# A one-core hybrid decoder layer: TensorE without extra transposes of the identity in its first waits

## The reference

```python
h = concatenate([meta_tokens, x])                 # 528 x 1024
hn = rms_norm(h, norm_mix_gain)
q, k, v, fg, glu_in, gate_a, gate_c = split(hn @ w_in)   # 3*1024, 16, 2048, 1024, 1024
a = forgetting_attention(q, k, v, fg + b_forget) @ w_attn_out
u = glu_in[:, :1024] * sigmoid(glu_in[:, 1024:])
c = silu(layer_norm(causal_depthwise_conv(u, 31 taps))) @ w_conv_out + b_conv_out
h = h + (sigmoid(gate_a) * a + sigmoid(gate_c) * c) @ w_out
h = h + square(relu(rms_norm(h) @ w_mlp_up)) @ w_mlp_down   # 1024 -> 4096 -> 1024
return rms_norm(h, final_norm_gain)[16:]
```

## Time and profile before

| | before |
|---|---|
| median of 3 runs | 928.09 us (927.62 to 929.64) |
| profiled execution, its own time | 928.93 us |
| its span, first to last instruction | 927.0 us |
| PE busy | 912.2 us, 98% |
| PE weight loads busy | 797.7 us, 86% |
| DVE busy | 622.8 us, 67% |
| ACT busy | 443.3 us, 48% |
| mean granted TensorE clock | 0.996 |

### The profile page before, as it was taken

The page is one execution under the profiler, slowest core; times in us unless marked ns, Lnnn a source line. Parts: engine busy times, 40 slices in busy tenths (PEclk is TensorE's granted clock), DMA queues, the critical chain, the costliest instruction groups (busy, mean ns, idle before and its releaser), DMA issues.

```text
span 927.0 us, 13909 instructions
## 1 busy us (share of the span) xinstructions
PE 912.2 (98%) x5138; PEld 797.7 (86%) x5138; DVE 622.8 (67%) x948; ACT 443.3 (48%) x709; POOL 30.3 (3%) x45
## 2 busy tenths in 40 slices
PE   8999999999999999998999999999999999999996
PEld 8999999899998988887888888888888888888886
DVE  7699989999999999976766656443444344334533
ACT  6432246777767767665842444421342134114312
POOL 2010000000000000031000000000000000000000
PEclk9999999999999999999999999999999999999999
DMA  8333332212221222222325333333233323333322
GB/s 244 109 94 93 90 91 70 69 48 69 68 68 46 74 63 68 70 69 68 102 80 190 105 90 92 91 92 107 86 104 94 109 85 97 94 110 88 94 69 92
DMA packets 153466, 84.35 MB, mean 91 GB/s; under 512 B 3039, under 2 KB 151519, under 8 KB 153424
## 3 DMA queue, kind: packets, MB, share of 16 engines
q1 hardware_dynamic: 152768, 83.37, 31.1%
q0 software_dynamic: 592, 0.29, 0.2%
q10 hardware_dynamic: 64, 0.13, 0.1%
HBM read 81.62 MB, written 2.16 MB: 90 GB/s over the span
## 4 chain that ended last, share of the span: by engine, by line
PE 89%; DVE 6%; ACT 3%; issue 1%; DMA 1%; ACTq 0%; DVEq 0%
PE pj L1237 61%; PE pj L1233 17%; PE pQ L1360 2%; PE pQ L1377 2%; DVE cv L908 2%; PE pj L1273 1%; PE pj L1515 1%; PE pQ L1347 1%; PE pQ L1346 1%; DVE cv L1100 1%; DVE w_lo L827 1%; DVE ga L1208 1%; ACT prob L591 1%; DVE prob L948 1%; ACT w_hi L515 1%
## 5 line engine op out<-in xcount | busy, mean ns | idle before, releaser
L515 ACT ACTIVATE w_hi<-raw 128x1024 fp32r<-128x1024 f32 x144 | 151.6, 1053 | 166.1 <-PE pj L1237 137.1
L827 DVE TENSOR_TENSOR w_lo<-raw,w_hi 128x1024 fp32r<-128x1024 f32 x144 | 175.9, 1221 | 43.2 <-ACT w_hi L515 42.8
L1237 PE MATMUL pj<-in_hi,w_hi 128*128 128x512 f32 x512 | 201.6, 394 | 2.5 <-DVE w_lo L827 2.4
L1237 PE MATMUL pj<-in_hi,w_lo 128*128 128x512 f32 x512 | 202.3, 395 | 0.0
L1237 PE MATMUL pj<-in_lo,w_hi 128*128 128x512 f32 x512 | 201.8, 394 | 0.0
L908 DVE SCALAR_TENSOR_TENSOR cv<-u,prm,cv 128x512 f32<-128x512 f32 x240 | 173.2, 756 | 0.5
L1237 PE MATMUL pj<-mid_hi,w_hi 128*128 128x512 f32 x368 | 144.4, 392 | 0.0
L1237 PE MATMUL pj<-mid_hi,w_lo 128*128 128x512 f32 x368 | 143.3, 389 | 0.0
L1237 PE MATMUL pj<-mid_lo,w_hi 128*128 128x512 f32 x368 | 143.2, 389 | 0.0
L1237 PEld LDWEIGHTS pj<-in_hi,w_hi 128*128 128x128 f32 x512 | 96.6, 189 | 23.1 <-DVE w_lo L827 2.8
L1237 PEld LDWEIGHTS pj<-in_lo,w_hi 128*128 128x128 f32 x512 | 96.6, 189 | 18.9 <-issue 0.5
(11 more groups left out here) (187 smaller groups left out, 1042.7 us busy)
## 6 DMA issues: line engine op xcount, KB each, us to landing
raw<-in_w_in_dram SPq DMA_DIRECT2D x57, 512.0 KB, 3.8
raw<-in_w_mlp_up_dram SPq DMA_DIRECT2D x32, 512.0 KB, 4.0
raw<-in_w_mlp_down_dram SPq DMA_DIRECT2D x32, 512.0 KB, 3.7
raw<-in_w_attn_out_dram SPq DMA_DIRECT2D x8, 512.0 KB, 3.7
raw<-in_w_conv_out_dram SPq DMA_DIRECT2D x8, 512.0 KB, 3.6
raw<-in_w_out_dram SPq DMA_DIRECT2D x8, 512.0 KB, 3.7
ga<-in_x_dram SPq DMA_DIRECT2D x4, 512.0 KB, 7.8
cv<-in_x_dram SPq DMA_DIRECT2D x1, 2048.0 KB, 9.0
```

Source lines behind the costliest of these rows:

```text
L515: A(w_hi[:, c % SPLIT, :], raw[:, c % RAW, :], ACT.Copy).then_inc(s_hi, 1)
L827: V.tensor_tensor(w_lo[:, c % SPLIT, :], raw[:, c % RAW, :], w_hi[:, c % SPLIT, :].bitcast(F32), ALU.subtract).then_inc(s_lo, 1)
L1237: last = mm(prod(c), wt, src[:, at:at + NT], **flags)
```

## The change

The function `keep_busy` and its three calls are left out. Nothing is put in their place; all waits, transposes and products of the tokens stay as they are and in the same order.

```diff
-            def keep_busy(n):
-
-                for _ in range(n):
-                    nc.tensor.transpose(pj[:, 0, 0:P], ident[:, :], ident[:, :])
-
...
             pe.wait_ge(s_const, 7)
-            keep_busy(20)
             tokens_transpose(0, ORDER[0])
-            keep_busy(4)
             tokens_transpose(1, ORDER[1])
-            keep_busy(12)
             tokens_transpose(2, ORDER[2])
             pe.wait_ge(s_par, 16 * 7)
```

## The result

The changed kernel is slower: 930.96 us against 928.9 us (medians of 18 runs each), a ratio of 1.0026 with a 95% interval of 1.0019 to 1.0033. That is 2.4 us (1.8 to 3.1); the medians by themselves differ by 2.1 us. One execution of each kernel took far longer than the others (3223 and 2342 us), and the ratio leaves these two out. Its profiled execution took 930.98 us, its span is 929.1 us (927.0 before).

A forecast was written before the change was run, and what follows sets the result against it. PE was taken to bound the kernel; 0.86 for slow tile 3 transposes plus 0.78 for slow products less 0.53 for the earlier start gave +1.1 us, on the median 928.09 thus 929.2 us, range 927.5 to 931.2.

The forecast's parts named there:

- The formula for the balance: Start of kernel: 0.86 us lost on tile 3, plus 0.46 per us from 16.4 to the clock's rise, less 0.53 gained.
- R: Moment at the start when PE's clock rises to the high level; taken as 18.1 us, giving +1.1 us.
- the same: Whole kernel: a time within 0.2%, 1.86 us, of before; chance 0.67.
- the first rival: First products of chunks 0 and 1: clock rises late, +2.5 to +3.9 us, 930.6 to 932.0 us; chance 0.20.
- PE has no pause worth the name from 11.70 on: From tile 2's transposes on, PE works on with only 0.2 us of pause before 14.69.
- the 4.9 us of the earlier trace: PE's work before the clock came back at 428.2 us; put R at 16.6 or 19.6, +0.4 or +1.8 us.
- 4.5 us without a pause did not suffice: First fill, 2.36 to 6.89 us: transposes at 9.31 were still spaced 0.214 us; used as support for a late rise.
- transposes don't count for the clock: Start of kernel: PE's work counts only from 16.40, +2.6 us, 930.7 us; chance 0.08.
- the clock doesn't hang on the fill: Start of kernel: clock rises by 11.8 us anyway, chunk 0 0.45 to 0.53 us earlier, 927.6 us; chance 0.07.
- The gain by a fall that goes away: Clock's fall at 424.8 us, costing 1.56 us, no longer occurs; with the start's gain -2.1 us, 926.0 us; chance 0.05.
- The fills' own cost: Start of kernel: without the fills tile 3's transposes can start at 14.69 for 15.22, a gain of 0.53 us.

The follow-up runs named there:

- bare_par: Kernel without the three fills, the parameters' eight small transposes moved behind tile 2's first half, five 128x128 identity transposes in their place; ratio 1.0014 to the kernel before.
- mid20: Kernel before, with 20 more identity transposes in the 2.4 us wait at 420.9 to 423.3 us; 927.03 us, ratio 0.9991.
- no12: Kernel before, with only the 12 extra transposes before tile 2 left out; 930.40 us, ratio 1.0022.
- no4: Kernel before, with only the 4 extra transposes between the meta tokens and tile 1 left out; 927.31 us, ratio 0.9999.
- early: Kernel before, with the identity made earlier and the first fill started near 1.4 us with 27 transposes for 20; 927.53 us, ratio 0.9992.
- prod: Kernel before, with each two extra transposes replaced by one float32 product of the identity with itself; 928.08 us, ratio 0.9999.
- only12: Changed kernel with only the 12 extra transposes before tile 2 put back; 928.76 us, ratio 1.0008 to the kernel before.
- no20: Kernel before, with only the first fill of 20 transposes left out; 928.34 us, ratio 1.0008.

## Why the prediction was wrong

**What held.** PE bounds the kernel and a shift at the start reaches the end in full: 1.96 us at tile 4, 2.1 in the span. The clock at the start was read rightly from the spacing, against the record. Tile 1 was forecast from 8.82, tile 2 from 11.70, tile 3 from 14.69; they came at 8.80, 11.83 and 14.77. Chunk 0 was forecast from 16.40 and came at 16.39; to the last hundredth that is luck, since tile 3 came 0.08 late and took 0.09 less. No load and no wait took the fill's place. The formula for the balance was right too: with the measured rise, 0.86 + 0.46 x (20.1 - 16.4) - 0.53 gives 2.0, and the trace has 0.77 for tile 3's transposes, 1.63 for the sixteen slow products (3.67 us for 2.04), less 0.45 for the earlier start: 1.95 us. The rest up to the 2.4 us of the ratio is open; it is within the interval.

**What failed is the size of one term, R, the moment of the rise.** The prediction took the middle of 16.6 and 19.6, R = 18.1, and so +1.1 us and "the same". It came at 20.1 in both profiles of this start, which is past the 19.7 from which the first rival, "the rise comes late", decides. The forecast lost and this rival came true, near its threshold: its price of +2.5 to +3.9 was too high, since its R of 21.1 to 24.1 was too late. The ratio of 1.0026 put on the 928.09 us of before gives 930.5, inside the range to 931.2. But 0.67 stood on no change, and the kernel is slower. The 2.0 us by which R was too early are 0.9 us of the time (0.46 x 2.0). Two steps led to it.

- "PE has no pause worth the name from 11.70 on" counted busy time alone. The eight small transposes of the parameters are busy time in the timeline, and in bare_par's profile, with wider ones in their place, the rise comes some 2.5 us sooner. Of the two values that the prediction had from the 4.9 us of the earlier trace rows, 16.6 and 19.6, the later one, with its +1.8 us, was near the mark; it was halved away. Why the rise comes when it does stays open beyond that.
- The prediction took the kernel's one profile for the kernel. The moments of rise and fall differ between executions of the same instructions (mid20's start against the earlier trace rows), so the loss is a mean over them. That "4.5 us without a pause did not suffice" holds of that one execution: in the profiles of no12, no4 and mid20 the same 20 transposes were enough, and the meta tokens' transposes behind them take 0.66 us for 1.03.

**The other rivals.** That transposes don't count for the clock is refuted: in early the clock rose within 27 of them by 6.3 us, and prod's products did no better that could be seen. The rule of the Trainium skill that the prediction weighed (TensorE: Matmul & The Clock Gate, Part 4: PE-mode transpose) thus stands against this case's traces twice. That the clock doesn't hang on the fill is refuted by the 0.239 us spacing after the change, and by no12. The gain by a fall that goes away did not come by the change: its profile has the fall. In mid20 a fill closes the wait before it, and the profile has none.

**The fills' own cost** was forecast as 0.53 us in all, to be won by leaving them out. It was won (0.45), and the 12 cost more where the clock is low through all of them (tile 2 at 13.39 in only12). They are worth it all the same.

## What to carry to other kernels

Before taking out work that nobody reads, find out whether it holds TensorE's clock: compare the start-to-start spacing of equal instructions before and after it. If it does, look at the waits that it closes one by one: here the last ones before the dense products were worth most, and the fill had to be long enough for the doubled pace too. A wait of a few us in the middle of a kernel that is otherwise bound by TensorE is worth the same try; here it gave about 0.8 us by itself, at the edge of what the runs can tell, and a clear 1.5 us together with the earlier start.

## What the runs showed of the hardware that was not expected

- The granted clock's record can be silent about the start: 1.00 in all stretches of the kernel of before, with transposes spaced 0.214 us up to 11.8 and 0.106 after it.
- The clock fell at 9.3 us in the profiles of no12 and no4 and at 9.75 in mid20's, while PE worked on tile 1. The last wait of over 0.9 us, before the meta tokens, was over by then (0.95, 1.07 and 1.58 us long). The clock was high again 3.4 us later where the 12 stood, and 10.2 us later in no12, where PE waited 1.34 us in their place and then worked for 7.8 us without a pause.
- The same wait of 2.4 us in mid-kernel led to a fall in the profiles of before and after and to none in those of no20, no4, early and bare_par.
- With eight transposes of 38x38 between wide ones the low spacing lasted to 20.1 us in two profiles, with five of 128x128 in their place to 17.5 us in one, though PE shows as busy in either.
